# Filling foreseen waits of TensorE with matmuls of ones, and splitting weights in smaller steps, in a fused three-block transformer kernel

## What is computed

```python
def first_block(x, ...):                       # one layer
    h = rms(x, norm_w) @ w_in                  # 8 parts: q, k, v, gate of two mixers
    oa = diff_attention(q, k, v, lam)          # 4 heads, two softmaxes, ALiBi
    orr = bidirectional_retention(qr, kr, vr)  # 4 heads, chunks of 128, both directions
    return x + concat(oa * silu(ga), orr * silu(gr)) @ w_out

def second_block(x, ...):                      # two layers
    x = x + mlstm_mixer(rms(x))                # 4 heads, chunks of 128, both directions
    x = x + swiglu(rms(x))
    x = x + window_attn_mixer(rms(x))          # rope, 16 query and 4 key heads, window 128, sink
    x = x + swiglu(rms(x))
    return rms(x)

def mlstm_mixer(h, ...):  # ... h_fwd + h_bwd, normalised, times sigmoid(output gate), @ w_out
def swiglu(h, w_in, w_out):
    gate, up = split(h @ w_in)
    return (silu(gate) * up) @ w_out
```

## Time and profile before

| | |
|---|---|
| median of 3 runs | 1494.66 us (1492.83 to 1494.66) |
| the profiled execution | 1491.64 us, of it a span of 1489.8 us from the first to the last instruction |
| PE busy in the span | 1455.9 us (98%) |
| PE weight loads | 1188.4 us (80%) |
| DVE busy | 783.2 us (53%) |
| ACT busy | 572.3 us (38%) |
| POOL busy | 51.0 us (3%) |
| mean granted clock of TensorE | 0.991 of full speed |

### The profile page before, as it was taken

The page is one execution under the profiler, slowest core; times in us unless marked ns, Lnnn a source line. Parts: engine busy times, 40 slices in busy tenths (PEclk is TensorE's granted clock), DMA queues, the critical chain, the costliest instruction groups (busy, mean ns, idle before and its releaser), DMA issues.

```text
span 1489.8 us, 18042 instructions
## 1 busy us (share of the span) xinstructions
PE 1455.9 (98%) x7202; PEld 1188.4 (80%) x7202; DVE 783.2 (53%) x1440; ACT 572.3 (38%) x1004; POOL 51.0 (3%) x108
## 2 busy tenths in 40 slices
PE   9999998999999799999999999998999999999997
PEld 8878765888888688888888887865678888888887
DVE  5665653566656764453345445677664443344443
ACT  5554542344444443232223233456743222223222
POOL 0011000000000000000000000001000000000000
PEclk9999999999999999999999999999999999999999
DMA  6211110231122022312322223210022322322221
GB/s 243 86 57 57 57 58 29 71 114 59 59 81 83 32 85 85 113 68 99 131 85 88 86 100 116 86 50 37 1 80 90 105 76 95 123 98 85 89 86 67
DMA packets 22035, 123.16 MB, mean 83 GB/s; under 512 B 2368, under 2 KB 4544, under 8 KB 10816
## 3 DMA queue, kind: packets, MB, share of 16 engines
q1 hardware_dynamic: 21952, 122.02, 23.8%
HBM read 119.91 MB, written 2.10 MB: 82 GB/s over the span
## 4 chain that ended last, share of the span: by engine, by line
PE 93%; DVE 3%; ACT 2%; issue 1%; DMA 1%; SPq 0%; DVEq 0%; POOLq 0%; POOL 0%; ACTq 0%
PE PS L247 85%; PE PS L269 5%; PE PS L277 3%; DVE WL L226 1%; DMA RAW<-in_w_in 1%; ACT WH L213 0%; DVE G L226 0%; DVE FT L235 0%; ACT FT L213 0%; DVE ACC L226 0%; DMA FT<-in_pos 0%; SPq L294 0%; DVE FP L235 0%; DVE FT L231 0%; DVE FT L226 0%
## 5 line engine op out<-in xcount | busy, mean ns | idle before, releaser
L247 PE MATMUL PS<-XH,WH 128*128 128x512 f32 x1080 | 430.0, 398 | 0.0
L247 PE MATMUL PS<-XH,WL 128*128 128x512 f32 x1080 | 420.8, 390 | 0.0
L247 PE MATMUL PS<-XL,WH 128*128 128x512 f32 x1080 | 420.6, 389 | 0.0
L247 PE MATMUL PS<-FR,WH 128*128 128x512 f32 (+1 forms) x1132 | 344.3, 387 | 8.6 <-DVE SC L231 2.7
L226 DVE TENSOR_TENSOR WL<-RAW,WH 128x1024 fp32r<-128x1024 f32 (+2 forms) x244 | 263.7, 1122 | 160.0 <-ACT WH L213 155.2
L213 ACT ACTIVATE WH<-RAW 128x1024 fp32r<-128x1024 f32 (+2 forms) x244 | 224.3, 967 | 145.1 <-PE PS L247 140.5
L247 PEld LDWEIGHTS PS<-FR,WH 128*128 128x128 f32 x1132 | 210.5, 190 | 52.6 <-issue 3.9
L247 PEld LDWEIGHTS PS<-XH,WH 128*128 128x128 f32 x1080 | 202.8, 188 | 47.1 <-issue 5.8
L247 PEld LDWEIGHTS PS<-XL,WH 128*128 128x128 f32 x1080 | 202.9, 188 | 42.6 <-issue 2.6
L247 PEld LDWEIGHTS PS<-XH,WL 128*128 128x128 f32 x1080 | 202.7, 188 | 42.8
L247 PE MATMUL PS<-FR,WL 128*128 128x512 f32 (+1 forms) x566 | 217.6, 384 | 0.0
(11 more groups left out here) (116 smaller groups left out, 1254.5 us busy)
## 6 DMA issues: line engine op xcount, KB each, us to landing
RAW<-in_f_in SPq DMA_DIRECT2D x44, 1024.0 KB, 4.7
RAW<-in_w_in SPq DMA_DIRECT2D x13, 1024.0 KB, 4.8
RAW<-in_m_in SPq DMA_DIRECT2D x12, 1024.0 KB, 4.8
RAW<-in_f_oa SPq DMA_DIRECT2D x16, 768.0 KB, 4.2
RAW<-in_f_ob SPq DMA_DIRECT2D x16, 640.0 KB, 3.8
RAW<-in_a_in SPq DMA_DIRECT2D x6, 1024.0 KB, 4.8
RAW<-in_w_out SPq DMA_DIRECT2D x4, 1024.0 KB, 4.8
RAW<-in_m_out SPq DMA_DIRECT2D x4, 1024.0 KB, 4.9
```

What stands on the lines that cost most here:

```text
L247: f = lambda e: e.matmul(o, l, r, start=start, stop=stop, skip_group_check=True)
```

## The change

Three edits, all in the planner and in what it queues.

First, `warm`: ahead of each matmul, `mm4` or transpose the planner compares the planned time of what it waits for with PE's planned clock. If PE would stand for 1.2 us or more, a free PSUM bank is there and 20 us of plan have gone by, int((idle - 0.5) / 0.22) matmuls of ones (128 x 128) into that bank are queued first. Their results are not read. That places 42 of them: 15, 20, 3 and 4.

Second, weight chunks are split in four quarters (128 x 512) in place of two halves, outside the FFNs (`smooth`). A chunk's quarters are kept in a list `parts`, and `feed` puts one on the queues after each second tile k of a projection or an output projection (or each fourth one), in place of a whole chunk at once. `w_upto` puts what is left when the chunk is needed.

Third, `soon` is no longer taken from its front: `weave` takes the entry that is due first. Gate activations, the mLSTM's gate scale and the split after a rope turn become entries of their own, put on their engine's queue only when their input is due.

```diff
@@ weave
         if soon:
-            can.append((due(soon[0][0]), -1))
+            at = min(range(len(soon)), key=lambda i: due(soon[i][0]))
+            can.append((due(soon[at][0]), -1))
...
-            soon.popleft()[1]()
+            fn = soon[at][1]
+            del soon[at]
+            fn()
@@ blocks_kernel
+    def warm(after):
+
+        idle = due(after) - PE.t
+        free = next((x for x in bank.q if due(x[1]) <= PE.t), None)
+        if idle < 1.2 or free is None or PE.t < 20:
+            return
+        for _ in range(int((idle - 0.5) / 0.22)):
+            PE.quiet(lambda e: e.matmul(PS[:, free[0], 0:128], ONE[:, :], ONE[:, :], start=True, stop=True,
+                                        skip_group_check=True), free[1], us=0.22)
+
     def mm(o, l, r, start, stop, *after, last=None):
+        warm(after)
...
     def mm4(o, l, r, start, stop, *after, last=None, us=None):
 
+        warm(after)
...
     def tr(o, i, ident, *after, last=True):
+        warm(after)
@@ w_prep
-        toks = []
-        n0 = (nk + 1) // 2
+        w_split[j] = []
+        cuts = [0, (nk + 1) // 2, nk] if not smooth[0] else list(range(0, nk, 2)) + [nk]
+        for a, b in zip(cuts, cuts[1:]):
+            parts.append((j, a, b))
+        if not smooth[0]:
+            w_upto(j)
...
+    def w_part():
+
+        j, a, b = parts.popleft()
+        ap, nk, wdt = chunks[j]
         free = w_done[j - 2] if j >= 2 else None
-        for a, b in ((0, n0), (n0, nk)):
-            r = RAW[:, j % 2, a * wdt:b * wdt]
-            toks.append(split(r, WH[:, j % 2, a * wdt:b * wdt], WL[:, j % 2, a * wdt:b * wdt],
-                              (wd[j % 2], 16 * ((j + 1) // 2)), free))
-        w_split[j] = toks
-        if w_at[0] == j + 2 and w_at[0] < len(chunks):
+        r = RAW[:, j % 2, a * wdt:b * wdt]
+        tok = split(r, WH[:, j % 2, a * wdt:b * wdt], WL[:, j % 2, a * wdt:b * wdt],
+                    (wd[j % 2], 16 * ((j + 1) // 2)), free)
+        w_split[j] += [tok] * (b - a)
+        if b == nk and w_at[0] == j + 2 and w_at[0] < len(chunks):
             w_load(w_at[0])
             w_at[0] += 1
...
+    def w_upto(j):
+        while parts and parts[0][0] <= j:
+            w_part()
+
+    def feed():
+        if parts:
+            w_part()
@@ w_use
+            if i == j:
+                w_upto(j)
@@ gate_tile
-        ready["g", g] = act(G[:, g, :], G[:, g, :], func, t1)
+
+        def gate():
+            t = act(G[:, g, :], G[:, g, :], func, t1)
+            if scale is not None:
+                soon.append((t, lambda: scaled(t)))
+            else:
+                ready["g", g] = t
+
+        def scaled(t):
+            ready["g", g] = ts(G[:, g, :], G[:, g, :], scale, ALU.mult, t, t_sm)
+
+        soon.append((t1, gate))
@@ out_proj
             t = piece(c, two[c], k, u)
+            feed()
...
                     t = piece(c, cur, k, u)
                     adds()
+                    if k % 2:
+                        feed()
@@ a_proj
-        def finish(key, u, x):
-            ready.setdefault(key + ("l",), []).append(rope2(x))
+        def turned(key, u, x):
+            f, tb = rope2(x)
+            soon.append((tb, lambda: finish(key, u, f, tb)))
+
+        def finish(key, u, f, tb):
+            got = ready.setdefault(key + ("l",), {})
+            got[u] = rope3(f, tb)
...
@@ the five parts
+    smooth[0] = True
     weave(chain(block1_proj(), out_proj(C_MIX0)), side1(), PE, bank, soon)
...
+    smooth[0] = False
+    w_upto(len(chunks))
     ffn(0, C_MIX1, a_rope_tables)
+    smooth[0] = True
...
+    smooth[0] = False
+    w_upto(len(chunks))
     ffn(1, C_FIN)
```

More of the change, by code:

```diff
@@ L342, in w_load @@
         WHEN[tok] = SP.t + 2.0
+    parts, smooth = deque(), [False]
     def w_prep(j):
         while w_at[0] < min(j + 2, len(chunks)):
-            if w_at[0] >= 2 and w_split[w_at[0] - 2] is None:
+            if w_at[0] >= 2 and not w_full(w_at[0] - 2):
                 break
@@ L350, in w_prep, with w_full @@
         ap, nk, wdt = chunks[j]
-        toks = []
-        n0 = (nk + 1) // 2
-        free = w_done[j - 2] if j >= 2 else None
-        for a, b in ((0, n0), (n0, nk)):
-            r = RAW[:, j % 2, a * wdt:b * wdt]
-            toks.append(split(r, WH[:, j % 2, a * wdt:b * wdt], WL[:, j % 2, a * wdt:b * wdt],
-                              (wd[j % 2], 16 * ((j + 1) // 2)), free))
-        w_split[j] = toks
-        if w_at[0] == j + 2 and w_at[0] < len(chunks):
+        w_split[j] = []
[4 more added lines that the diff above has]
+            w_upto(j)
+    def w_full(j):
+        return w_split[j] is not None and len(w_split[j]) == chunks[j][1]
+    def w_part():
+        j, a, b = parts.popleft()
+        ap, nk, wdt = chunks[j]
+        free = w_done[j - 2] if j >= 2 else None
+        r = RAW[:, j % 2, a * wdt:b * wdt]
[3 more added lines that the diff above has]
+        if b == nk and w_at[0] == j + 2 and w_at[0] < len(chunks):
             w_load(w_at[0])
             w_at[0] += 1
+    def w_upto(j):
[4 more added lines that the diff above has]
+            w_part()
     w_next = [0]
@@ L374, in w_use @@
         l = WL[:, j % 2, 0:nk * wdt].rearrange("p (k n) -> p k n", n=wdt)
-        return j, h, l, [w_split[j][k * len(w_split[j]) // nk] for k in range(nk)]
+        return j, h, l, w_split[j]
     t_x, t_w0, t_n1 = [], [], None
@@ L458, in proj_tm @@
                     (h[:, k, 0:256], l[:, k, 0:256]), k == 0, k == KT - 1, wt[k], xs[k], fb)
+            if k % 4 == 3:
+                feed()
         st["pt"] = t
@@ L496, in prep_all @@
             part = slice(512 * i, 512 * i + 512)
-            w_split[0].append(split(RAW[:, 0, part], WH[:, 0, part], WL[:, 0, part], t_w0[i]))
+            w_split[0] += 2 * [split(RAW[:, 0, part], WH[:, 0, part], WL[:, 0, part], t_w0[i])]
             prep_parts(2 * i, wcol)
@@ L503, in blocks_kernel, with gate_tile @@
     ready = {}
-    def gate_tile(b, t, g, func):
+    def gate_tile(b, t, g, func, scale=None):
         t1 = tt(G[:, g, :], PS[:, b, :], RB[:, :], ALU.mult, t, st["rbt"], st.get(("g", g)))
@@ L1201, in m_proj @@
                     g = 2 * hd + u
-                    gate_tile(b, t, g, ACT.Sigmoid)
-                    ready["g", g] = ts(G[:, g, :], G[:, g, :], SM[:, C_MLN + g:C_MLN + g + 1], ALU.mult, ready["g", g], t_sm)
+                    gate_tile(b, t, g, ACT.Sigmoid, SM[:, C_MLN + g:C_MLN + g + 1])
                 w_done[j] = t
@@ L1372, in m_turn @@
     def m_turn(hd, i, f, tok):
-        while ("g", 2 * hd + 1) not in ready:
+        while ("g", 2 * hd) not in ready or ("g", 2 * hd + 1) not in ready:
             yield None
@@ L1442, in rope2, with rope3 @@
         ft.put(g, tb)
+        st["rope_read"] = [ta, tb]
+        return f, tb
+    def rope3(f, tb):
         fh, f1 = fr.take()
@@ L1446, in rope2 @@
         ft.put(f, tk)
-        st["rope_read"] = [ta, tb]
         return fh, fl, tk
@@ L1453, in a_proj @@
         ready["nsk"] = (nsk, ts(nsk, SM[:, C_SINK:C_SINK + 16], -1.0, ALU.mult, t_sm))
-        def finish(key, u, x):
-            ready.setdefault(key + ("l",), []).append(rope2(x))
+        def turned(key, u, x):
[4 more added lines that the diff above has]
+            got[u] = rope3(f, tb)
             held[0] -= 1
-            if u == 1:
-                ready[key] = ready[key + ("l",)]
+            if len(got) == 2:
+                ready[key] = [got[0], got[1]]
         def roped(key, u, x):
             held[0] += 1
-            soon.append((x[3], lambda: finish(key, u, x)))
+            soon.append((x[3], lambda: turned(key, u, x)))
         for c in A_ORDER:
```

## The result

| | before | after |
|---|---|---|
| median | 1493.74 us (1490.57 to 1494.66, 4 runs) | 1482.96 us (1482.14 to 1483.84, 4 runs) |
| ratio, 95% interval | | 0.9934 (0.9920 to 0.9949) |
| the profiled execution, its span | 1491.64, 1489.8 us | 1483.84, 1482.1 us |
| mean granted clock | 0.991 | 0.996 |

By the medians the change makes the kernel 10.8 us faster (7.6 to 12.0 by the interval), where 5.0 was forecast for the likeliest case; the time lies inside the stated range near its low end, where the prediction had its second rival (11 us, "more goes than I count").

A forecast was written before the change was run, and what follows sets the result against it. TensorE was taken as the bound (busy 1455.9 of 1489.8 us), its long waits also lowering the clock. 2.7 + 1.0 + 1.3 = 5.0 us off gave 1489.7 us against the median of three runs, range 1482 to 1496.

The forecast's parts named there:

- second rival: Quarters shorten the chains where ACT and DVE pace PE, so more waits go: 11 us, 1483.6 us; chance 0.17.
- Part 1: Ones at the end of the first block's projections keep the clock up: gain 2.7 us, between -3 and 4.5.
- The first and the fourth rival: First: waits only filled, 1494.8 us, chance 0.23. Fourth: ones overshoot, 1500.6 us, 0.10 together with pieces ahead of heads' chains.
- the second fall at 1081.57: Attention's last split: with the wait cut to 1.1 to 1.3 us, even chance the clock stays, +0.8 us.
- Part 2: Quarters for halves outside the FFNs: extra DVE time lies beside PE work, 0 us, up to 6 lost.
- signs of being wrong: Ones of 0.4 us each, a clock still falling there, or new PE waits for DVE in 60-180 or 960-1080.
- Part 3: Start of the mLSTM's output projection: fewer split pieces in DVE's chain, gain 1.0 us, between -2 and 4.5.
- Part 4: Attention phase: longer first wait filled by ones, shorter last wait, later third weight chunk: gain 1.3 us, between -4 and +6.
- No part: Rope tables' stretch at 902.72 keeps its 1.92 us wait and low clock; last tile's 7 ones lie inside waits.
- third rival: Falls of the clock move to other waits: 1488.0 or 1491.4 us, inside the forecast's range; chance 0.50 together with the forecast.

The follow-up runs named there:

- e1: The changed kernel without the 42 matmuls of ones, quarters and order by due times kept: 1486.82 us.
- e3: The changed kernel with weight chunks split in halves as before, ones and order by due times kept: 1483.00 us.
- e4: The kernel before with only the order by due times and the deferred gate, scale and rope steps, no ones, halves: 1484.06 us.
- e8: e3 with the rope tables' positions loaded into a buffer of their own half an FFN earlier: 1476.76 us.
- e11: The changed kernel (quarters, ones, order) with the positions for the rope tables loaded early: 1480.26 us.
- e5: e4 with the gate's activation and the mLSTM's scale put on their queues at once again: 1488.17 us.

## Why the prediction held, and where it didn't

**Part 1, the ones: right.** Forecast were 2.7 and 1.66 us, 4.4 together; taking them away cost 3.9, and adding them to before won 4.4. By stages they won 3.2 and 2.1 us (e1 to after). Their price (0.22 us for one; 0.23 to 0.24 measured), that they end before what they wait for, that they shorten no wait and that the clock holds, all came as put. The first and the fourth rival fall: the waits are not only filled, and the ones run at full clock. The even chance given to the second fall at 1081.57 can't be judged from one profile, since with the wait of 1.82 us the clock fell there in 2 of 6. The first block as a whole won 1.9 us, less than the 2.7, because the quarters cost 1.6 there.

**Part 2, the quarters: the zero was too kind.** They win nothing in any of the three pairs (0.0, -2.8 and -3.5 us). The profiles place the loss. The first block is 1.6 us longer with quarters in each pair (e3 to after, e4 to e1, e8 to e11). The mLSTM is 0.6 and 0.8 us longer in the last two, where the falls can be compared, and the attention phase 2.3 and 0.7, the 2.3 from the longer wait (4.66 against 2.28 us). The profile of e3, in the first pair, had costly falls in the mLSTM and at the rope tables that after's did not have, which hides the loss there. In the first block one new wait of PE for DVE shows, at 125.12 us, and such a wait between 60 and 180 was one of the signs of being wrong:

```profile
125.12 0.98 PE L261 MATMUL PS<-FR 64*128 64x512 f32 x6 [0.37 <-DVE FR L229]
```

The other 1.2 us are spread over many matmuls, in steps too small for a row, and their cause stays open. DVE is busy for 6.3 to 7.1 us longer with quarters, within the 5 to 18 of the forecast; that it lies beside PE's work is what did not hold in full.

**Part 3, the mLSTM's output projection: the size near, the step wrong.** 1.0 us was forecast because one quarter would stand ahead of the chain and one inside it. DVE's timeline of after shows six quarters there:

```profile
494.89 1.29 DVE L229 TENSOR_TENSOR WL<-RAW,WH 128x512 fp32r<-128x512 f32 x2
...
497.62 2.48 DVE L229 TENSOR_TENSOR WL<-RAW,WH 128x512 fp32r<-128x512 f32 x4
```

1.29 + 2.48 = 3.8 us where the halves took 2.36. On DVE the quarters take 1.4 us more at this place, and the stage loses 0.6 to 0.8 us by them; the scales and their waits, 2.4 us, win more. So 1.0 lies near the measured 1.8 by luck. I had written that the scale "stood among them before too", and did not look at the 0.70 us that DVE stood ahead of each. e5 shows that this is the part's gain. The lower end that I gave this part, for a new fall of the clock, was wrong too: the fall did come (0.83 in 490 to 500), and the mLSTM still gained 1.8 us, since DVE sets the pace at that place, as in e4.

**Part 4, the attention phase: the sum was too small, 1.3 against 4.3 us.** The wait ahead of the first output piece is filled to its end by the ones, as forecast. What was mis-sized: the waits of 0.91, 0.65 and 0.40 us, which had no term, gave way to one of 0.69; the wait before the last split is 0.93 us, not 1.1 to 1.3; and the new wait for the third chunk, put at 0.8 us, is some 0.2: its first quarter is done at 1085.42 + 0.7 = 1086.1 us, and PE has work until 1086.0. PE had 9 triples left when the additions began (1079.9 to 1086.0 us at 0.68), not 8. That both falls of the phase are gone is worth 3.3 us, of which the sum had 2.5.

One step stands ahead of all these. e4, with no ones and no quarters, has the whole gain of the phase (215.22 us, against 215.41 in after). The forecast took the wait of 4.16 us for a copy behind a weight split. It did not look at the rope's split one row ahead, for which ACT stood 2.88 us; putting that split later is worth 2.5 us, and the sum has no term for it. The 2.1 us that the ones win here go into the longer wait that the quarters make.

**No part: half right.** The wait at the rope tables stayed. Its fall of the clock did not show in the first profile and showed in the second, which is the third rival, and as small as it was put there.

So the sum of 5.0 us fell 5.8 short of the medians. 3.0 of that is the scatter of the two profiled executions. Of the other 2.8, 3.0 lie in the attention phase; the first block (0.8 under the forecast), the mLSTM (0.8 over it) and the draws at the start and at the rope tables nearly cancel. The reason is one above all: the third edit, taken as a mere means, was worth more than the other two (8.6 us alone, by the medians). Each step of it that I priced, I priced by its duration; its worth lies in what stands behind it on its queue.

## What to carry to other kernels

On an in-order queue, look at the wait in front of an instruction before its duration: a step that is queued before its input is ready stops everything behind it, and putting it later can be worth more than making it shorter. Matmuls of ones in a foreseen wait of TensorE are worth the low clock that they prevent, if they fill the wait nearly to its end (0.5 us left was little enough here, 2.2 was not) and if TensorE sets the pace behind it. Smaller pieces are no gain by themselves: here they won nothing in one pair and cost about 3 us in two. And before a difference of 1 or 2 us is explained, compare the stages: two profiles with the same order in a stage show what is only a draw of the clock.

## What the runs showed of the hardware

The same wait of 2.02 us in two executions of one program left the clock at 1.00 once and at 0.83 once, so at such a place a single profile shows only one draw. At the two places where the ones stand it was no draw: with 2.2 us or more of bare wait the clock fell in 19 cases of 19, and with 0.55 us or less in none of 9. Over the runs of before the mean granted clock went from 0.988 to 0.994, and the times with it from 1494.99 to 1488.37 us. And a stretch at half rate, 20 matmuls in 7.65 instead of 4.79 us, cost nothing where VectorE was the slower engine (11.38 against 11.30 us for the whole place); a fall some 12 us later in the same sequence of instructions cost 1.5 us (263.97 and 263.99 us for the stage against 262.48).
